# A two-branch diffusion trunk: where the second attention's scores, maxima and first exponential stand between the gate's pieces, and one wait in the last layer's pair products

## The chip, the core and the metric

The kernel runs on one core of one Trainium2 chip. The metric is the device time of one execution in microseconds (us), median of three runs. The core has TensorE (PE in the rows; PEld is its weight load), VectorE (DVE), ScalarE (ACT), GpSimd (POOL) and SyncE (SP), which here only issues DMAs. Each has its own queue of instructions in program order; they wait for each other by semaphores.

## What is computed

Two token streams (512 latent and 128 context tokens, 640 columns in the kernel) pass through two layers. A layer has one combined input projection, four branches (latent attention, gated DeltaNet, Hyena convolution, differential attention), a sigmoid gate for each branch and channel, a projection, a residual, and an MLP. The parts that the change touches, cut from the reference:

```python
def _diff_attend(q, k, v, lam):          # the second attention: two maps for each head
    ...
        s1 = jnp.einsum('bqhd,bkhd->bhqk', qb[..., 0, :], k1).astype(jnp.float32) * scale
        s2 = jnp.einsum('bqhd,bkhd->bhqk', qb[..., 1, :], k2).astype(jnp.float32) * scale
        p = jax.nn.softmax(s1, axis=-1) - lam * jax.nn.softmax(s2, axis=-1)
        return jnp.einsum('bhqk,bkhd->bqhd', p.astype(v.dtype), v)

def _gated_merge(branches, z_gate, w_branch, w_out):
    stacked = jnp.stack(branches, axis=2)
    proj = jnp.einsum('blnc,ncd->blnd', stacked, w_branch)
    gates = jax.nn.sigmoid(z_gate.reshape(bsz, seq, N_BRANCH, D_MODEL))
    return jnp.einsum('bld,de->ble', jnp.sum(gates * proj, axis=2), w_out)

def _trunk_layer(x, p, l, cond, ctx):
    ...
    x = x + gt_m * (jnp.square(jax.nn.relu(h @ p['mlp_w1'][l])) @ p['mlp_w2'][l])
```

## The kernel before, in words

**Attention and gates share one stretch.** The two attentions are cut into 40 units, each one head and one tile of 128 queries: units 0 to 19 are the first attention (one map of scores), units 20 to 39 the second (two maps). Two units of one tile (an even and an odd one, two neighbouring heads) make a pair; the last tile of each five is the context's, with 128 columns of scores instead of 640 (units 18 and 19, 28 and 29, 38 and 39). A unit v goes through the engines so: PE multiplies queries and keys (`score`; for two maps twice two matmuls into the two halves of `ps_aux`, L1708, or L1705 for a context unit); DVE takes each map's maximum (`row_max`, L3065); ACT takes each map's exponential with its sum (`exp`, L2288); DVE scales and combines them (`combine`, L3074 for one map, L3081 to L3086 for two); PE transposes the result (`turn`, L1723); ACT copies it out of `ps_dense` (`turned`, L2298); and after each odd unit PE multiplies both with the values (`values`, L1735).

**Between these stand the gate's pieces.** 22 of the 32 gate blocks are computed inside the attentions. A block i has five pieces (i, 0) to (i, 4), called `gate_part`: pieces 0 to 3 are 12 matmuls of 320 columns each (L1035), piece 3 also the rows of the modulation (L1061), and piece 4 turns those rows (L1068) and projects a branch (L1657). On ACT a block has a copy of the projection's weights (L2055, at piece 1), a copy of the next block's weights (L2050, at piece 2) and the tanh of the gate (L2276, at piece 3); on DVE it has the copy of the rows (L3193, at piece 3), which L1068 reads, and the product of gate and projection (L3046, at piece 4), which frees the bank for the next block's piece 0. In the second attention each pair carries one block: pieces 0 and 1 in the even unit's step, 2 and 3 in the odd unit's, 4 behind it. The order is written by hand, in one loop on each engine; a helper only says which pieces stand in which step.

**What a step of unit v holds.** On PE: the pieces, then `score(v + 1)`, then `turn(v)`; only where an even unit's step holds a piece 4 does the score come first, which never is the case in the second attention. On ACT: the pieces, the first map's exponential of v + 1, `turned(v)`, the second map's exponential of v + 1. On DVE: the pieces, `row_max(v + 1)`, `combine(v + 1)`.

**What a score waits for.** Each map of unit v + 1 overwrites the half of `ps_aux` that the same map of unit v used, so it waits for that map's exponential:

```python
                                pe.wait_ge(*exps.nth(l, U + 2 * u - 1 + m))
```

It also waits for its tile's queries, which SP loads (L773) after the weights of a later gate block (L752), when piece 4 of the pair two places before is done.

**The MLP's pairs.** In the MLP, 14 pairs of hidden blocks in each layer are computed by seven quadrant products each (`quadrant_pair`), with operands split into high and low parts. In the even pairs (seven of the 14) a function `early` is called between products 4 and 5; in the first layer it computes rows of the next layer's modulation, in the last layer it returns at once. Ahead of the call PE waits for the low part of operand A22, which product 7 needs; DVE makes it (L3300). Products 5 to 7 wait for DVE's sums of the quadrants (L3327 and after).

Of the kernel before, what the change touches and what calls it, by code (L numbers as in the profile page):

```python
# [23 lines left out]
DEPTH = 2  # L24
# [147 lines left out]
def trunk(nc, ins, outs, links):  # L172
    ctx = ExitStack()
    with ctx:
# [96 lines left out]
        parts = sums  # L271
# [225 lines left out]
        U = NT * H  # L497
# [208 lines left out]
        def has_branch(parts):  # L706

            return any(q % 5 == 4 for q in parts)
# [312 lines left out]
        def _(pe):  # L1021
# [660 lines left out]
            def attention(l):  # L1682
# [78 lines left out]
                for w in range(U):  # L1761
                    for v in (2 * w, 2 * w + 1):
                        parts = parts_ahead(3 * w + v % 2)
                        score_first = v % 2 == 0 and has_branch(parts)
                        if score_first:
                            score(v + 1)
                        for q in parts:
                            gate_part(l, q)
                        if v + 1 < 2 * U and not score_first:
                            score(v + 1)  # L1770
                        turn(v)
                    for q in parts_ahead(3 * w + 2):
                        gate_part(l, q)
                    values(w)
# [162 lines left out]
            def mlp_group(l, g):  # L1937
# [19 lines left out]
                        dense_split(dense_banks(j % 2), j % 2, h_high, h_low, block_low(l, 0, j))  # L1957
                for p in range(first_pair(g), (g + 1) * GROUP_PAIRS):
                    i = p % GROUP_PAIRS
                    quadrant_pair(l, p, (lambda: early(i // 2)) if i % 2 == 0 and (g or i) else None)  # L1960
                last_pair = (g + 1) * GROUP_PAIRS - 1
                for m in range(KC):
                    pe.wait_ge(*block_high(l, g, KC + m))
# [51 lines left out]
        def _(act):  # L2015
# [262 lines left out]
            def attention(l):  # L2278
# [40 lines left out]
                a(q_high.bitcast(F32R), d_q, ACT.Copy).then_inc(parts_ready.sem, 1)  # L2319
                for w in range(U):  # L2320
                    for v in (2 * w, 2 * w + 1):
                        for q in parts_ahead(3 * w + v % 2):
                            gate_part(l, q)
                        two = v + 1 < 2 * U and FU[v + 1][0] == 2
                        if two:
                            exp(v + 1, 0)
                        turned(v)
                        if v + 1 < 2 * U:
                            exp(v + 1, 1 if two else 0)
                    for q in parts_ahead(3 * w + 2):  # L2330
                        gate_part(l, q)
# [224 lines left out]
        def _(dve):  # L2556
# [499 lines left out]
            def attention(l):  # L3056
# [46 lines left out]
                for w in range(U):  # L3103
                    for v_ in (2 * w, 2 * w + 1):
                        parts, behind = parts_ahead(3 * w + v_ % 2), parts_ahead(3 * w + 2)
                        score_first = v_ % 2 == 0 and has_branch(parts)
                        if score_first:
                            row_max(v_ + 1)
                        for q in parts:
# [519 lines left out]
```

## Time and profile before

| | |
|---|---|
| median of 3 runs | 2722.15 us (2717.51 to 2723.63) |
| profiled execution, its own time | 2714.22 us |
| its span | 2712.4 us |
| PE busy | 2593.4 us (96%) |
| PEld busy | 2415.4 us (89%) |
| DVE busy | 1373.8 us (51%) |
| ACT busy | 981.1 us (36%) |
| POOL busy | 666.5 us (25%) |
| PE's share of the chain that ended last | 83% |

Busy is the time in which an engine had an instruction under way, as a share of the span. The profiled execution took 2714.22 us, 7.93 us less than the median of the runs and 3.29 us less than the fastest of them; a sum made from its rows is a difference, and is added to the median. The chain that ended last follows the work back from the last instruction, at each step to what released it.

### The profile page before, as it was taken

The numbers are of one execution on the slowest core, as the hardware profiler recorded it, in microseconds if no ns is written. First come the engines' busy times: TensorE is split into PE (matmuls) and PEld (weight loads), VectorE is DVE, ScalarE is ACT, GpSimd is POOL, SyncE is SP. The second block draws the span as 40 slices with busy tenths as digits, with TensorE's granted clock in tenths as the row PEclk, the third lists the DMA queues.
The fourth block names the chain that finished last, engine by engine and source line by source line (L and its number), as shares of the span: only waits on it lengthen the run. The fifth ranks groups of instructions, "written<-read, shape, count | busy, mean of one in ns | idle before, by whom it ended". The sixth has DMA issues, their size and how long they took to land.

```text
span 2712.4 us, 55055 instructions
## 1 busy us (share of the span) xinstructions
PE 2593.4 (96%) x23766; PEld 2415.4 (89%) x23766; DVE 1373.8 (51%) x2295; ACT 981.1 (36%) x1590; POOL 666.5 (25%) x525
## 2 busy tenths in 40 slices
PE   5998999999999999999999989999999999999997
PEld 5887897889899999999988888888898998999997
DVE  5767624236633646255575775342464347364364
ACT  4251043334422534253341511443344226253352
POOL 2322122222233220211323311322222331211202
PEclk8999999999999999999999999999999999999999
DMA  8110012433343123222330100134332431122222
GB/s 347 40 55 3 3 59 87 142 107 104 108 131 128 63 92 111 83 97 102 131 132 32 48 4 11 62 120 130 99 115 100 143 105 63 63 86 79 74 83 78
DMA packets 73148, 245.38 MB, mean 90 GB/s; under 512 B 7828, under 2 KB 20276, under 8 KB 71888
## 3 DMA queue, kind: packets, MB, share of 16 engines
q1 hardware_dynamic: 69936, 218.21, 23.7%
q0 software_dynamic: 2976, 23.69, 2.4%
q8 instruction: 189, 3.10, 0.5%
q14 instruction: 47, 0.39, 0.0%
HBM read 224.66 MB, written 17.20 MB: 89 GB/s over the span
## 4 chain that ended last, share of the span: by engine, by line
PE 83%; DVE 6%; ACT 5%; issue 3%; DMA 1%; POOL 0%; SPq 0%; DVEq 0%; ACTq 0%; POOLq 0%
PE ps_dense L1027 29%; PE ps_dense L1035 17%; PE ps_dense L1890 5%; PE ps_aux L1027 4%; PE ps_dense L1657 3%; PE ps_dense L1894 3%; PE ps_aux L1421 2%; PE ps_dense L1735 1%; PE ps_aux L1657 1%; PE ps_aux L1711 1%; PE ps_dense L1061 1%; PE ps_aux L1407 1%; PE ps_dense L1723 1%; PE ps_aux L1373 1%; DMA arena<-in_w_early 1%
## 5 line engine op out<-in xcount | busy, mean ns | idle before, releaser
L857 POOL TENSOR_TENSOR w_low<-w_ring,w_high 128x256 fp32r<-128x256 f32 (+1 forms) x338 | 515.7, 1542 | 1450.6 <-ACT w_high L2050 1444.3
L2050 ACT ACTIVATE w_high<-w_ring 128x1024 fp32r<-128x1024 f32 x200 | 212.1, 1061 | 460.2 <-PE ps_dense L1027 260.5
L1027 PE MATMUL ps_dense<-z_both,w_high 128*128 128x320 f32 x2048 | 312.5, 310 | 0.0
L1027 PEld LDWEIGHTS ps_dense<-z_both,w_high 128*128 128x128 f32 x2048 | 302.6, 188 | 2.1 <-issue 1.6
L1035 PE MATMUL ps_dense<-h_high,w_high 128*128 128x320 f32 x1024 | 242.2, 318 | 7.1 <-DVE x_res L3043 3.1
L1035 PE MATMUL ps_dense<-h_high,w_low 128*128 128x320 f32 x1024 | 233.2, 309 | 0.0
L1035 PE MATMUL ps_dense<-h_low,w_high 128*128 128x320 f32 x1024 | 232.5, 308 | 0.0
L3187 DVE SCALAR_TENSOR_TENSOR x_res<-ps_dense,mod,x_res 128x320 f32<-128x320 f32 (+2 forms) x192 | 72.6, 434 | 292.2 <-PE ps_dense L1027 292.2
L1027 PE MATMUL ps_dense<-h_high,w_high 128*128 128x320 f32 x864 | 204.5, 318 | 14.8 <-ACT h_high L2091 11.4
L1027 PE MATMUL ps_dense<-h_low,w_high 128*128 128x320 f32 x864 | 186.8, 309 | 0.0
L1035 PEld LDWEIGHTS ps_dense<-h_high,w_high 128*128 128x128 f32 x1024 | 167.8, 188 | 14.5 <-issue 12.6
L1035 PEld LDWEIGHTS ps_dense<-h_low,w_high 128*128 128x128 f32 x1024 | 171.1, 188 | 0.0
L1035 PEld LDWEIGHTS ps_dense<-h_high,w_low 128*128 128x128 f32 x1024 | 171.0, 188 | 0.0
L1027 PEld LDWEIGHTS ps_dense<-h_high,w_high 128*128 128x128 f32 x864 | 146.1, 192 | 27.5 <-issue 13.8
L1027 PE MATMUL ps_dense<-z_both,w_low 128*128 128x320 f32 x1024 | 160.6, 309 | 0.0
L1027 PEld LDWEIGHTS ps_dense<-z_both,w_low 128*128 128x128 f32 x1024 | 152.8, 188 | 0.0
L1027 PE MATMUL ps_dense<-h_high,w_low 128*128 128x320 f32 x864 | 147.6, 313 | 0.0
L3193 DVE COPY rows_kept<-ps_dense 128x128 f32<-128x128 f32 x64 | 18.7, 292 | 247.1 <-ACT stage L2276 132.4
L1027 PEld LDWEIGHTS ps_dense<-h_low,w_high 128*128 128x128 f32 x864 | 141.7, 188 | 0.3 <-issue 0.3
L1027 PEld LDWEIGHTS ps_dense<-h_high,w_low 128*128 128x128 f32 x864 | 134.1, 191 | 0.0
L3065 DVE TENSOR_REDUCE att_s<-ps_aux 128x1 f32<-128x640 f32 (+1 forms) x120 | 82.2, 713 | 83.3 <-PE ps_aux L1711 40.6
L1890 PE MATMUL ps_dense<-h_low,w_high 128*128 128x320 f32 x392 | 117.9, 312 | 0.0
(528 smaller groups left out, 5084.5 us busy)
## 6 DMA issues: line engine op xcount, KB each, us to landing
w_ring<-in_w_mlp SPq DMA_DIRECT2D x128, 512.0 KB, 3.6
w_ring<-in_w_gate SPq DMA_DIRECT2D x64, 640.0 KB, 3.9
w_ring<-in_w_late SPq DMA_DIRECT2D x64, 512.0 KB, 4.9
w_ring<-in_w_in SPq DMA_DIRECT2D x48, 512.0 KB, 3.5
w_ring<-in_w_out SPq DMA_DIRECT2D x16, 512.0 KB, 3.5
w_ring<-in_w_early SPq DMA_DIRECT2D x16, 512.0 KB, 3.5
arena<-in_dft POOLq DMA_DIRECT2D x2, 2944.0 KB, 14.9
x_kept<-x_res POOLq DMA_DIRECT2D x2, 2560.0 KB, 11.9
```

The costliest lines, as they stand in the source:

```text
L857: last = g.tensor_tensor(w_low[:, n % 2, k:k + step], ring[:, slot, k:k + step, :], w_high[:, n % 2, k:k + step].bitcast(F32), ALU.subtract)
L1027: last = mm(out[:, s, 0:HALF], w_[:, par_, k, :], x_[:, k, s * HALF:(s + 1) * HALF], start=first, stop=final)
L1035: last = mm(out[:, s, 0:HALF], w_[:, par_, k, :], x_[:, k, s * HALF:(s + 1) * HALF], start=k == 0 and x_ is x_high and w_ is w_high, stop= ...
L1061: last = mm(out[32 * (k % 4):32 * (k % 4) + 32], cond_pad[:, k, at:at + 32], tiles[:, k, :], start=j == 0 and k < 4, stop=j == of - 1 and ...
L1373: return mm(psA[to, 2 * i, u * 64:(u + 1) * 64], lt[s % 3][rows(r), d, hh, rows(r)], mv, start=True, stop=True)
L1421: last = mm(out, wm[i][at, u], mv, start=not moved, stop=True)
L1657: last = mm(out[:, s, 0:HALF], w_[:, k, :], x_[:, k, s * HALF:(s + 1) * HALF], start=n == 0 and k == 0, stop=n == 2 and k == 1)
L1890: mm(out, w_[:, k // 2, k % 2], src[:, k], start=fresh and k == 0 and n == 0, stop=False, skip_group_check=True)
L1894: last = mm(out, rest[:, k // 2, k % 2], b_high[:, k], start=False, stop=k == 3, skip_group_check=True)
L2050: a(w_high[:, n % 2], ring[:, j, 0:KC, :], ACT.Copy).then_inc(w_high_in.sem, 1)
L3065: v.tensor_reduce(small_[:, 2 * m, u:u + 1], src, AX.XY if len(src.shape) == 3 else AX.X, ALU.max, negate=True).then_inc(negmax.sem, 1)
L3187: last = v.scalar_tensor_tensor(out=dst[:, p:q], in0=ps, scalar=gate[:, s:s + 1], in1=dst[:, p:q], op0=ALU.mult, op1=ALU.add)
```

## The change

In the second attention the step of every unit is put in another order, on three engines. PE computes `score(v + 1)` ahead of the gate's pieces of step v, for v from 19 to 38; DVE takes the maxima of unit v + 1 ahead of its pieces; ACT takes the first map's exponential of unit v + 1 ahead of its pieces. In the last layer, `quadrant_pair` gets no `early` function, and so PE no longer waits for A22's low part between products 4 and 5. No instruction is added and none removed but that wait.

```diff
@@ TensorE, attention
                         parts = parts_ahead(3 * w + v % 2)
-                        score_first = v % 2 == 0 and has_branch(parts)
+                        score_first = U <= v + 1 < 2 * U or v % 2 == 0 and has_branch(parts)
                         if score_first:
                             score(v + 1)
                         for q in parts:
@@ TensorE, mlp_group
                     i = p % GROUP_PAIRS
-                    quadrant_pair(l, p, (lambda: early(i // 2)) if i % 2 == 0 and (g or i) else None)
+                    quadrant_pair(l, p, (lambda: early(i // 2)) if i % 2 == 0 and (g or i) and l + 1 < DEPTH else None)
@@ ScalarE, attention
                     for v in (2 * w, 2 * w + 1):
-                        for q in parts_ahead(3 * w + v % 2):
-                            gate_part(l, q)
                         two = v + 1 < 2 * U and FU[v + 1][0] == 2
                         if two:
                             exp(v + 1, 0)
+                        for q in parts_ahead(3 * w + v % 2):
+                            gate_part(l, q)
                         turned(v)
@@ VectorE, attention
                         parts, behind = parts_ahead(3 * w + v_ % 2), parts_ahead(3 * w + 2)
-                        score_first = v_ % 2 == 0 and has_branch(parts)
+                        score_first = U <= v_ + 1 < 2 * U or v_ % 2 == 0 and has_branch(parts)
                         if score_first:
                             row_max(v_ + 1)
```

**PE, from an even unit's transposes to the odd unit's pieces.** These are PE's rows in the second attention's second pair (units 22 and 23) before. The four L1708 are the scores of the odd unit, two matmuls for each map; the L1723 are the transposes of the even unit; the L1035 begin piece 2. `exps` is the semaphore of the exponentials, `stacked_queries_in` that of the loaded queries.

```order
L1708 MATMUL ps_aux<-z_both,q_stack_odd 128x320 [waits exps,stacked_queries_in,stacked_keys_in]
L1708 MATMUL ps_aux<-z_both,q_stack_odd 128x320
L1708 MATMUL ps_aux<-z_both,q_stack_odd 128x320 [waits exps]
L1708 MATMUL ps_aux<-z_both,q_stack_odd 128x320
L1723 MATMUL ps_dense<-con,arena 128x128 [waits probabilities_ready,pv_in,pt_in]
L1723 MATMUL ps_dense<-con,arena 128x128 x4
L1035 MATMUL ps_dense<-h_high,w_high 128x320 x2
```

And the same place of the changed kernel:

```order
L1723 MATMUL ps_dense<-con,arena 128x128 [waits probabilities_ready,pv_in,pt_in]
L1723 MATMUL ps_dense<-con,arena 128x128 x4
L1708 MATMUL ps_aux<-z_both,bout_low 128x320 [waits exps,stacked_queries_in,stacked_keys_in]
L1708 MATMUL ps_aux<-z_both,bout_low 128x320
L1708 MATMUL ps_aux<-z_both,bout_low 128x320 [waits exps]
L1708 MATMUL ps_aux<-z_both,bout_low 128x320
L1035 MATMUL ps_dense<-h_high,w_high 128x320 x2
```

The odd unit's scores have left this place for the start of the even unit's step, and the scores of the next pair's even unit (queries in `bout_low`) now stand directly behind the transposes, with pieces 2 and 3 behind them instead of ahead of them.

**PE, from the modulation's rows to their transpose.** The same pair before, at the end of piece 3 (L1061) and the start of piece 4 (L1068):

```order
L1061 MATMUL ps_dense<-w_ring,cond_pad 32x128 x7
L1708 MATMUL ps_aux<-z_both,bout_low 128x320 [waits exps,stacked_queries_in,stacked_keys_in]
L1708 MATMUL ps_aux<-z_both,bout_low 128x320
L1708 MATMUL ps_aux<-z_both,bout_low 128x320 [waits exps]
L1708 MATMUL ps_aux<-z_both,bout_low 128x320
L1723 MATMUL ps_dense<-con,arena 128x128 [waits probabilities_ready,pt_in]
L1723 MATMUL ps_dense<-con,arena 128x128 x4
L1068 MATMUL ps_dense<-con,rows_kept 128x2 [waits modulation_rows_in,gate_act]
```

Changed:

```order
L1061 MATMUL ps_dense<-w_ring,cond_pad 32x128 [waits ring_in3]
L1061 MATMUL ps_dense<-w_ring,cond_pad 32x128 x7
L1723 MATMUL ps_dense<-con,arena 128x128 [waits probabilities_ready,pt_in]
L1723 MATMUL ps_dense<-con,arena 128x128 x4
L1068 MATMUL ps_dense<-con,rows_kept 128x2 [waits modulation_rows_in,gate_act]
```

Between L1061 and L1068, which waits for tanh (`gate_act`) and the rows' copy (`modulation_rows_in`), only the transposes are left.

**ACT, one pair.** Before, from piece 1 on; `negmax` is DVE's maximum:

```order
L2055 ACTIVATE w_proj_high<-w_ring 128x256 [waits block_done]
L2288 ACTIVATE arena,att_s<-ps_aux,att_s 128x640 [waits negmax]
L2298 ACTIVATE arena<-ps_dense 128x640 [waits pv_ps,pt_ps]
L2288 ACTIVATE arena,att_s<-ps_aux,att_s 128x640 [waits negmax]
L2050 ACTIVATE w_high<-w_ring 128x1024 [waits block_done,ring_in0]
L2276 ACTIVATE stage<-ps_dense 128x640 [waits proj_used,gate_ps]
```

Changed:

```order
L2055 ACTIVATE w_proj_high<-w_ring 128x256 [waits block_done]
L2298 ACTIVATE arena<-ps_dense 128x640 [waits pv_ps,pt_ps]
L2288 ACTIVATE arena,att_s<-ps_aux,att_s 128x640 [waits negmax] x2
L2050 ACTIVATE w_high<-w_ring 128x1024 [waits block_done,ring_in0]
L2276 ACTIVATE stage<-ps_dense 128x640 [waits proj_used,gate_ps]
```

The first exponential has gone ahead of L2055, and the next unit's first exponential stands ahead of the weights' copy L2050; the copy out of `ps_dense` (L2298) and the second exponential keep their order to each other.

## Rows read from the trace of the kernel before

**Rows 1.** Busy time by engine in most of the first layer's second attention.

```profile
core 0: us, PE busy (x) PEld busy (x) DVE busy (x) ACT busy (x) POOL busy (x), PEclk, DMA share, GB/s
614.00:748.00 134.00, 130.78 (x1098) 121.64 (x1096) 82.26 (x180) 57.96 (x126) 39.07 (x50) 1.00 0.32 107
```

**Rows 2.** Who waited for whom, 600 to 755: us in total, times, longest.

```profile
PE ps_dense L1068 <- DVE rows_kept L3193: 2.3, 5, 1.0
PE ps_dense L1035 <- DVE rs L3046: 1.3, 2, 0.6
```

**Rows 3.** Timeline, second attention: start, duration, engine, instruction, [idle before it].

```profile
646.19 1.56 DVE L3065 TENSOR_REDUCE att_s<-ps_aux 128x1 f32<-128x640 f32 x2 [1.57 <-PE ps_aux L1708]
646.29 0.71 PE L1723 MATMUL ps_dense<-con,arena 128*128 128x128 f32 x5
646.75 0.54 PE L1035 MATMUL ps_dense<-h_high,w_high 128*128 128x320 f32 x2
647.05 0.80 ACT L2288 ACTIVATE arena<-ps_aux,att_s 128x640 f32<-128x640 f32 x1 [5.21 <-DVE att_s L3065]
...
647.84 0.70 ACT L2298 ACTIVATE arena<-ps_dense 128x640 f32<-128x640 f32 x1
...
648.42 0.80 ACT L2288 ACTIVATE arena<-ps_aux,att_s 128x640 f32<-128x640 f32 x1
...
649.19 1.07 ACT L2050 ACTIVATE w_high<-w_ring 128x1024 fp32r<-128x1024 f32 x1
...
649.34 0.16 DVE L3084 RECIPROCAL att_s<-att_s 128x1 f32<-128x1 f32 x1 [0.62 <-ACT arena L2288]
...
649.79 0.89 DVE L3086 SCALAR_TENSOR_TENSOR arena<-arena,att_s 128x640 f32<-128x640 f32 x1
...
650.45 0.64 PE L1061 MATMUL ps_dense<-w_ring,cond_pad 128*32 128x128 f32 x16
...
651.02 0.86 PE L1708 MATMUL ps_aux<-z_both,q_stack_odd 128*128 128x320 f32 x4
651.16 0.70 ACT L2276 ACTIVATE stage<-ps_dense 128x640 f32<-128x640 f32 x1 [0.90 <-PE ps_dense L1061]
...
651.89 0.29 DVE L3193 COPY rows_kept<-ps_dense 128x128 f32<-128x128 f32 x1 [1.22 <-ACT stage L2276]
...
652.33 0.35 PE L1068 MATMUL ps_dense<-con,rows_kept 128*128 128x2 f32 x2
...
655.73 0.56 PE L1035 MATMUL ps_dense<-h_high,w_high 128*128 128x320 f32 x2
```

**Rows 4.** SP's load of queries: one issue, and the eight loads' time to landing.

```profile
641.81 0.38 SPq L773 DMA_DIRECT2D q_stack_odd<-q_parts  x1
...
DMA to landing us min/median/max: 5.0/5.8/6.6
```

**Rows 5.** Timeline at the context's units, where the second attention begins.

```profile
605.94 0.54 PE L1035 MATMUL ps_dense<-h_high,w_high 128*128 128x320 f32 x2
...
606.93 0.16 DVE L3074 RECIPROCAL att_s<-att_s 128x1 f32<-128x1 f32 x1 [0.53 <-ACT par L2288]
...
614.73 0.53 PE L1035 MATMUL ps_dense<-h_high,w_high 128*128 128x320 f32 x2 [0.64 <-DVE rs L3046]
```

**Rows 6.** Timeline, last layer's MLP: A22's low part, and where product 5 starts.

```profile
2508.54 0.69 DVE L3300 TENSOR_TENSOR con_reused<-w_ring,par_reused 128x512 fp32r<-128x512 f32 x1
...
2513.73 0.49 DVE L3327 TENSOR_TENSOR flow<-flow,ps_dense 128x320 f32<-128x320 f32 x1
...
2514.32 0.39 PE L1890 MATMUL ps_dense<-h_high,w_high 128*128 128x320 f32 x1 [0.95 <-issue]
```

**Rows 7.** Last layer's first pair, start of product 5, and the stretches behind it.

```profile
2296.56 0.38 PE L1890 MATMUL ps_dense<-h_high,w_high 128*128 128x320 f32 x1 [2.35 <-issue]
...
2297.70:2301.00 3.30, 3.30 (x14) 3.30 (x14) 2.25 (x4) 1.89 (x3) 0.00 (x0) 0.50 0.90 309
2302.00:2305.30 3.30, 3.30 (x24) 3.30 (x24) 2.52 (x5) 1.51 (x4) 0.00 (x0) 1.00 0.02 9
```

## The prediction, on record before the changed kernel ran

> **What bounds the kernel now.** I read the windows first, then PE's waits, then the timeline. The window over the first layer's second attention shows PE with an instruction under way for 130.78 of 134.00 us, at full granted clock, while DVE has 82.26 and ACT 57.96 [rows 1]: PE sets the pace, and whatever makes PE stand still or puts nothing in place of a moved matmul is time. The waits say how little there is to win here. In 155 us, PE waited 2.3 us for the copy of the modulation's rows (five times) and 1.3 us for the gate's product on DVE (twice) [rows 2]. With both layers that is 7.2 us, and all of PE's idle time in the window, 134.00 - 130.78 = 3.2 us, says about the same. The timeline of one pair then shows how PE came to wait so seldom [rows 3]: it is always busy with a piece of the gate while DVE and ACT work on the softmax. Each map of a unit takes one maximum on DVE and one exponential on ACT, and ACT has the copy out of ps_dense between the two exponentials.
>
> **The change in the odd unit's step: the scores lose their cover.** Take the pair in [rows 3]. The even unit's transposes start on PE at 646.29, and piece 2 at 646.75. In the changed order the scores of the next pair's even unit stand between these two. Their second map overwrites the half of ps_aux that the odd unit's second exponential reads, so PE waits for that exponential, and it stands on ACT behind the copy of the very transposes that PE has just made. The chain, from rows:
>
> - transposes end: 646.29 + 0.71 = 647.00 [rows 3]. ACT starts some 0.05 us behind an end on PE (L1061 ends at 650.45 + 0.64 = 651.09, and its tanh starts at 651.16), so the copy starts at 647.05 rather than at 647.84, where the first exponential held it up;
> - the second exponential starts 648.42 - 647.84 = 0.58 us behind the copy's start [rows 3], so at 647.63;
> - its result is released 649.34 - 648.42 = 0.92 us after its start (DVE's L3084 waits for just that) [rows 3], so at 648.55;
> - PE needs 0.05 more and half a score. A whole score takes 651.02 to 651.6, about 0.6 us with what stands ahead of L1723, so piece 2 starts near 648.9.
>
> Piece 2 would start at 648.9 instead of 646.75, which is 2.15 us later. Of this about 0.3 us is the first map's half, 0.3 the second's, and 1.55 is PE standing still.
>
> **Is that given back where the scores used to be?** Before, they stood between the modulation's rows (L1061, at 650.45) and the transpose of those rows (L1068, at 652.33). That distance is 1.88 us [rows 3], and it is not made of PE's work: L1061 takes until 651.09, tanh starts at 651.16 and takes 0.70, the copy of the rows starts at 651.89 and takes 0.29, and PE follows. The scores and transposes only just filled it, with what remained appearing as the five waits of 2.3 us in all [rows 2]. Without the scores PE has 0.6 us less to do there and waits 0.6 us longer; the distance stays 1.88. So nothing comes back, and a pair is longer by the full 2.15 us.
>
> **The even unit's step.** The odd unit's scores now stand ahead of pieces 0 and 1 instead of behind. What they wait for, the even unit's second exponential, was already done before: the projection and the values lie between, 652.33 to 655.73 [rows 3]. No wait, no gain, except at the two places in each layer where PE waits 0.64 us for the gate's product ahead of piece 0 because the values of a context pair are short [rows 5]. There the scores (0.6) fill the wait. That is 0.6 us won, twice in each layer.
>
> **Maxima and the first exponential.** They come earlier and are not what PE waits for: the first exponential of the odd unit started at 647.05, and DVE can start the maximum as soon as its queue lets it. What the move puts at risk is what stands behind the exponential on ACT, the weights' copy L2050 and tanh L2276. In the odd step the combination on DVE (L3084 to L3086: 0.45 + 0.89) runs after the release at 648.55, to 649.9; the maximum and the exponential's start take 647.05 - 646.19 = 0.86 more, to 650.8; the exponential 0.8, to 651.6, and the weights' copy 1.07, to 652.7. The rows (L1061) are now made at 648.9 + 3.7 = 652.6 (650.45 - 646.75 = 3.7), so tanh is wanted at 653.3. It fits with 0.6 us to spare: cost nothing, and if that cover is gone, each us beyond it costs one us a pair. POOL makes the low weights behind L2050, which ended at 650.26, 5.5 us before the next block's piece 0 at 655.73 [rows 3]; now it ends at 652.7 and that piece comes near 658, again more than 5 us. SP's queue keeps its order and all its transfers.
>
> **The queries.** A pair's queries are loaded behind piece 4 of the pair two places before: issued at 641.81, landed 5.8 us later at 647.6 (the eight loads take 5.0 to 6.6) [rows 4]. The new place asks for them at 646.75, so the first map now waits for a DMA that was hidden: to 647.6, less than the 648.55 of the second map's wait. Only the slowest loads reach past it: 6.6 us gives 648.4 plus the first half's 0.3, 0.15 us late. I count 0.2 us a layer.
>
> **The context's units and the first one.** Unit 28 and unit 38 have scores of 128 columns, behind full exponentials: 2.0 us each. Unit 30's scores stand behind the short unit 28; the exponential is early and the queries decide (0.9 us by the short chain, 2.15 by the long): 1.5. The very first, unit 20's scores, stand behind unit 18's transposes and wait for unit 19's exponential, which is released at 606.93 where piece 2 began at 605.94 [rows 5]: 1.0 us, and 0.6 for the scores, whose old place is one of those 1.88 us: 1.6.
>
> **The last layer's pairs.** PE's wait for A22's low part ends with DVE's L3300 at 2508.54 + 0.69 = 2509.2, and PE gets to it near 2513.4 and waits until 2514.32 for the first quadrant sum, DVE's L3327, 2513.73 + 0.49 = 2514.22 [rows 6]. The idle 0.95 us has another cause, and the removed wait was long satisfied. Worth nothing, in all seven pairs.
>
> **The sum.** For a layer: six full units (22, 24, 26, 32, 34, 36) by 2.15 = 12.9; two context scores by 2.0 = 4.0; 1.5; 1.6; 0.2 for queries; less 1.2 won. That is 19.0, and 38.0 us for two layers, on a profiled execution of 2714.2 which gives 2752.2. The median of the runs shown stands 7.9 us above that execution: 2722.15 + 38 = 2760. The unknown in it is how late each hand-over between PE and ACT is; 0.1 us either way on two hand-overs for each of 20 stalls is 4 us. The likeliest case's own range is 2753 to 2768. A measurement of this kernel can tell about 0.2%, 5.4 us, from no change.
>
> **Rivals.**
> - *The clock falls.* PE stood still once for 2.35 us, between 2294.2 and 2296.5, and the granted clock was then 0.50 (1.2 of 2.4 GHz) from 2297.70 to 2301.00: 14 matmuls in 3.30 us, where 24 passed at 1.00 [rows 7]. Ten matmuls lost are 3.30 x 10/24 = 1.4 us. After a wait of 0.95 us no fall is seen [rows 6, 1]. Mine are 1.55 us with 0.3 us of matmuls ahead and transposes before that, between the two. If each of 20 stalls brought the fall: 28 us more, 2788. For it: the new stalls are longer than any in this stretch. Against: matmuls stand densely on both sides. Chance 10%, part of the stalls only (2770 to 2788) in most of that. [...]
> - *Tanh comes late.* If the maximum of the next unit comes more than 0.6 us later than I have it, the first exponential and the weights' copy hold up tanh, the rows' transpose and piece 4. One us beyond is one us in each of 16 pairs of both layers: 2776. For it: DVE is the busiest of the helpers, 82.26 of 134 us [rows 1]. Against: the slack worked out above. Chance 7%.
> - *Not slower.* The second map's exponential would have to be released by the time PE has done the first half, 647.05, instead of 648.55; then the scores cost nothing in their new place, and the filled waits show, 1.2 us a layer, and at the most all of PE's 7.2 us of waits: 2715 to 2720. It decides at a release before 647.1, that is, if ACT's second exponential did not need the copy of the transposes ahead of it. In the order of ACT it stands behind it, which speaks against. Chance 5%.
> - *The stall is smaller*, because part of the 1.88 us is PE's work after all and comes back: 0.6 x 16 = 10 us less, 2750. For it: PE's waits for the rows are only 2.3 us. Chance 8%.
>
> The likeliest case holds the remaining 70%. The range reaches from the smaller stall to tanh late: 2747 to 2778. Faster by over 0.2%: 2%; within 0.2%: 3%; slower: 95%.
>
> **What the changed kernel's profile would show.** PE idle ahead of the second half of L1708 in the odd steps, about 1.5 us, released by ACT's L2288; its idle time in the stretch up from 3.2 us to above 20; L1068's wait for L3193 near 0.7 us in every pair; the distance L1061 to L1068 still 1.88; the wait of 0.64 us ahead of piece 0 gone; granted clock 1.00 throughout; the MLP's waits unchanged, 0.95 us ahead of product 5. A pair takes 2.15 us more. Wrong would be the prediction if L1068 or tanh moved by their own, or if the second exponential stood ready when PE reached it.

## The result

The changed kernel takes 2768.86 us, the median of 4 runs (2759.49 to 2776.35); the kernel before took 2721.22 us beside it (4 runs, 2717.51 to 2723.63). The ratio is 1.018, with a 95% interval of 1.016 to 1.0199: 47.6 us slower. Forecast were 38 us more and a time of 2760 with a range of 2747 to 2778. The four runs of the changed kernel lie 16.9 us apart, and the slower one is, the lower its mean granted clock: 0.992, 0.991, 0.989 and 0.988 at 2759.49, 2765.84, 2771.88 and 2776.35 us. The profiled execution is the second of them, 3.0 us below the median.

**The page of the changed kernel.** Its head and its first part, busy time by engine:

```profile
span 2764.1 us, 55055 instructions
PE 2606.9 (94%) x23766; PEld 2420.3 (88%) x23766; DVE 1372.0 (50%) x2295; ACT 983.7 (36%) x1590; POOL 663.0 (24%) x525
```

The number of instructions is the same as before, the span is 51.7 us longer. PE is busy for 13.5 us more although it does the same matmuls, and 12.8 us of that lie in the two second attentions. The granted clock is one part of it: in the three pairs where it fell to half (below), PE is busy for 1.9 to 2.1 us more. But in the pairs without a fall, the last one excepted, it is busy for 0.2 to 0.6 us more as well. There the rows ahead of a wait count for longer: one matmul's row lasts some 0.3 us and the next one starts some 0.15 us behind it, so a row that nothing follows shows its whole length. The rest of the 51.7 us, 38.2 us, is PE standing still.

**The first layer's second attention**, the window that answers to [rows 1] (the pairs are longer, so it runs to 768), and the first five rows of PE's waits from 600 to 785, which answer to [rows 2] (us in total, times, longest):

```profile
614.00:768.00 154.00, 134.87 (x1077) 122.28 (x1078) 80.94 (x180) 59.73 (x128) 35.99 (x50) 0.99 0.28 93
```

```profile
PE ps_dense L1068 <- DVE rows_kept L3193: 7.6, 12, 1.0
PE ps_aux L1708 <- ACT arena L2288: 6.2, 5, 2.6
PE ps_aux L1708 <- issue: 2.5, 3, 1.0
PE ps_aux L1705 <- issue: 1.7, 1, 1.7
PE ps_aux L1708 <- DMA z_both<-k_parts: 1.4, 1, 1.4
```

PE stands still for 154.00 - 134.87 = 19.1 us here; before it was 3.2. Two kinds of wait are new. The scores (L1708, and L1705 for the context) now wait in front of the odd units' pieces, and the rows' transpose L1068, which waited five times before, waits in every pair.

**One pair** as the timeline shows it, beside [rows 3]:

```profile
652.83 0.38 SPq L773 DMA_DIRECT2D q_stack_odd<-q_parts  x1
...
656.36 0.80 ACT L2288 ACTIVATE arena<-ps_aux,att_s 128x640 f32<-128x640 f32 x1 [5.70 <-DVE att_s L3065]
...
657.27 0.71 PE L1723 MATMUL ps_dense<-con,arena 128*128 128x128 f32 x5
...
658.02 0.70 ACT L2298 ACTIVATE arena<-ps_dense 128x640 f32<-128x640 f32 x1 [0.47 <-PE ps_dense L1723]
...
658.62 0.79 ACT L2288 ACTIVATE arena<-ps_aux,att_s 128x640 f32<-128x640 f32 x1
658.62 0.53 PE L1708 MATMUL ps_aux<-z_both,q_stack_odd 128*128 128x320 f32 x2 [0.64 <-issue]
...
659.55 0.56 PE L1708 MATMUL ps_aux<-z_both,q_stack_odd 128*128 128x320 f32 x2 [0.39 <-ACT arena L2288]
659.95 0.46 PE L1035 MATMUL ps_dense<-h_high,w_high 128*128 128x320 f32 x2
```

Read it from the transposes. They end at 657.98, the copy of them (L2298) starts at 658.02, the second exponential 0.60 us behind it, and 0.93 us after that PE may overwrite the second half of `ps_aux`, at 659.55. Piece 2 follows at 659.95, which is 2.68 us behind the start of the transposes; in [rows 3] it was 0.46. The first half waits as well, until 658.62. That is 5.79 us behind SP's issue at 652.83, so the queries had just landed. Here it costs nothing, since the second half would wait until 659.55 anyway.

**Pair by pair.** From the start of one pair's values (L1735) to the next, the changed kernel minus the one before, in us (the name is that of the even unit whose scores stand in the odd step of that stretch; "unit 22's pair" below means its row here):

| scores of | forecast | first layer | second layer |
|---|---|---|---|
| unit 20 | 1.6 | 1.68 | 1.68 |
| unit 22 | 1.55 | 5.59 | 5.59 |
| unit 24 | 2.15 | 2.14 | 2.13 |
| unit 26 | 2.15 | 2.09 | 2.09 |
| unit 28 (context) | 2.0 | 1.96 | 1.96 |
| unit 30 | 1.5 | 1.68 | 1.62 |
| unit 32 | 1.55 | 1.73 | 3.82 |
| unit 34 | 2.15 | 2.16 | 2.12 |
| unit 36 | 2.15 | 2.13 | 2.13 |
| unit 38 (context) | 2.0 | 2.14 | 1.97 |
| last pair | 0 | 0.01 | 0.01 |
| sum (forecast: with 0.2 for queries) | 19.0 | 23.3 | 25.1 |

Three cells are off, and they hold nearly all of the difference to the forecast. The pair with unit 22's scores, first layer, in the timeline:

```profile
620.87 1.49 DVE L3135 TENSOR_TENSOR bout_low<-bout,con_reused 128x1280 fp32r<-128x1280 f32 x1
621.61 0.71 PE L1723 MATMUL ps_dense<-con,arena 128*128 128x128 f32 x5
622.29 0.82 DVE L3054 TENSOR_TENSOR x_res<-x_res,rs 128x640 f32<-128x640 f32 x1
623.02 1.55 DVE L3065 TENSOR_REDUCE att_s<-ps_aux 128x1 f32<-128x640 f32 x2
623.87 0.79 ACT L2288 ACTIVATE arena<-ps_aux,att_s 128x640 f32<-128x640 f32 x1 [8.60 <-DVE att_s L3065]
...
624.90 0.53 PE L1708 MATMUL ps_aux<-z_both,q_stack_odd 128*128 128x320 f32 x2 [2.58 <-ACT arena L2288]
...
626.48 0.69 PE L1708 MATMUL ps_aux<-z_both,q_stack_odd 128*128 128x320 f32 x2 [1.05 <-ACT arena L2288]
```

Once in each layer DVE splits a branch's output into high and low parts (`split_branch(2)`, L3134 and L3135) behind the first attention's last pair, and a residual sum (L3054) follows. Unit 21's maxima stand behind both in DVE's queue and start at 623.02, 1.41 us after the start of the transposes. So even the first exponential comes late: PE waits 2.58 us for it and 1.05 us for the second. Behind that the granted clock falls, and in the second layer it falls behind unit 32's scores too:

```profile
626.90:630.20 3.30, 3.30 (x15) 3.30 (x14) 2.35 (x3) 1.64 (x3) 0.00 (x0) 0.50 0.00 0
...
2067.30:2070.60 3.30, 3.30 (x14) 3.30 (x14) 1.95 (x3) 1.83 (x3) 0.14 (x1) 0.50 0.00 0
```

```profile
2066.76 1.05 PE L1708 MATMUL ps_aux<-z_both,bout_low 128*128 128x320 f32 x4 [2.06 <-DMA z_both<-k_parts]
```

The last row names the keys' load, but of the loads that this score waits for, the queries' is the late one: SP issued it at 2060.33, 6.4 us before 2066.76, and the four issues of keys behind it are the context's, which unit 32 does not ask for. In the first layer the same wait was 1.43 us (the load issued at 698.67, the scores at 704.47), and no fall came. Here PE waited for 2.06 us, and then the clock was 0.50 (1.2 of 2.4 GHz) for 3.4 us.

**The MLP.** The row that answers to [rows 6], in the same pair, which now comes 51.5 us later:

```profile
2565.85 0.41 PE L1890 MATMUL ps_dense<-h_high,w_high 128*128 128x320 f32 x1 [0.90 <-DVE flow L3327]
```

The idle time is 0.90 us where it was 0.95, and it is now put down to DVE's sum.

**Where the 51.7 us of span lie.** The two second attentions hold 23.3 + 25.1 = 48.4. Some 1.6 us stand before the first of them and 1.5 between the two, in code that the change does not touch. Ahead of the first, the clock fell for three stretches of 3.4 us in this execution and for one in that of before; the long low stretch near the start of both lasted 10.2 us here and 13.6 us there. Between the two attentions the clock was low for 10.2 us in both, and where those 1.5 us come from stays open.

### The profile page after: what moved, and what is told of

It is laid out like the page before. It is cut to its first block, busy times and chain, and to the rows that moved or that the text cites. A ratio compares the mean times of both kernels' runs of the same rounds, so it can differ in the third digit from the quotient of the medians.

```text
span 2764.1 us, 55055 instructions
## 1 busy us (share of the span) xinstructions
PE 2606.9 (94%) x23766; PEld 2420.3 (88%) x23766; DVE 1372.0 (50%) x2295; ACT 983.7 (36%) x1590; POOL 663.0 (24%) x525
## 3 DMA queue, kind: packets, MB, share of 16 engines
q1 hardware_dynamic: 69936, 218.21, 23.3%
## 4 chain that ended last, share of the span: by engine, by line
PE 79%; DVE 7%; ACT 6%; issue 4%; DMA 2%; POOL 1%; SPq 1%; DVEq 0%; ACTq 0%; POOLq 0%
PE ps_dense L1027 29%; PE ps_dense L1035 15%; PE ps_aux L1027 4%; PE ps_dense L1890 4%; PE ps_dense L1657 3%; PE ps_dense L1894 2%; PE ps_aux L1421 2%; PE ps_dense L1735 1%; PE ps_aux L1657 1%; PE ps_aux L1711 1%; PE ps_dense L1061 1%; PE ps_aux L1407 1%; PE ps_aux L1373 1%; ACT flow L2433 1%; PE ps_aux L1708 1%
## 5 line engine op out<-in xcount | busy, mean ns | idle before, releaser
L2050 ACT ACTIVATE w_high<-w_ring 128x1024 fp32r<-128x1024 f32 x200 | 211.8, 1059 | 462.0 <-PE ps_dense L1027 260.5
L1027 PE MATMUL ps_dense<-z_both,w_high 128*128 128x320 f32 x2048 | 312.5, 310 | 0.0
L1027 PEld LDWEIGHTS ps_dense<-z_both,w_high 128*128 128x128 f32 x2048 | 302.6, 188 | 2.1 <-issue 1.6
L1035 PE MATMUL ps_dense<-h_high,w_high 128*128 128x320 f32 x1024 | 241.3, 317 | 4.6 <-DVE x_res L3043 3.1
L1035 PE MATMUL ps_dense<-h_high,w_low 128*128 128x320 f32 x1024 | 234.9, 311 | 0.0
L1035 PE MATMUL ps_dense<-h_low,w_high 128*128 128x320 f32 x1024 | 234.5, 310 | 0.0
L1027 PE MATMUL ps_dense<-h_high,w_high 128*128 128x320 f32 x864 | 203.4, 317 | 16.3 <-ACT h_high L2091 12.7
L1027 PE MATMUL ps_dense<-h_low,w_high 128*128 128x320 f32 x864 | 187.0, 309 | 0.0
L1035 PEld LDWEIGHTS ps_dense<-h_high,w_high 128*128 128x128 f32 x1024 | 170.5, 190 | 8.7 <-issue 6.4
L1035 PEld LDWEIGHTS ps_dense<-h_low,w_high 128*128 128x128 f32 x1024 | 172.9, 190 | 0.0
L1035 PEld LDWEIGHTS ps_dense<-h_high,w_low 128*128 128x128 f32 x1024 | 172.8, 190 | 0.0
L1027 PEld LDWEIGHTS ps_dense<-h_high,w_high 128*128 128x128 f32 x864 | 144.7, 190 | 29.0 <-issue 15.0
L1027 PE MATMUL ps_dense<-z_both,w_low 128*128 128x320 f32 x1024 | 160.6, 309 | 0.0
L3193 DVE COPY rows_kept<-ps_dense 128x128 f32<-128x128 f32 x64 | 18.6, 291 | 283.0 <-ACT stage L2276 168.4
L1027 PEld LDWEIGHTS ps_dense<-z_both,w_low 128*128 128x128 f32 x1024 | 152.8, 188 | 0.0
L1027 PE MATMUL ps_dense<-h_high,w_low 128*128 128x320 f32 x864 | 146.4, 312 | 0.0
L1027 PEld LDWEIGHTS ps_dense<-h_low,w_high 128*128 128x128 f32 x864 | 141.8, 188 | 0.3 <-issue 0.3
L1027 PEld LDWEIGHTS ps_dense<-h_high,w_low 128*128 128x128 f32 x864 | 133.1, 190 | 0.0
L865 POOL TENSOR_TENSOR w_ring_low<-w_ring,w_proj_high 128x256 fp32r<-128x256 f32 x64 | 53.0, 828 | 256.3 <-ACT w_proj_high L2055 256.3
```

Source lines behind the costliest of these rows:

```text
L865: g.tensor_tensor(ring_low[:, at, KC:KC + 2, :], ring[:, at, KC:KC + 2, :], w_proj[:].bitcast(F32), ALU.subtract)\
L1027: last = mm(out[:, s, 0:HALF], w_[:, par_, k, :], x_[:, k, s * HALF:(s + 1) * HALF], start=first, stop=final)
L1035: last = mm(out[:, s, 0:HALF], w_[:, par_, k, :], x_[:, k, s * HALF:(s + 1) * HALF], start=k == 0 and x_ is x_high and w_ is w_high, stop= ...
L2050: a(w_high[:, n % 2], ring[:, j, 0:KC, :], ACT.Copy).then_inc(w_high_in.sem, 1)
```

## The experiments

Where it is not said otherwise, a kernel computes all that the reference asks for. Differences by pair are always against the trace of the kernel before, of one execution each. The edits of the first two sections are shown against the kernel before, the others against the changed kernel, and all are cut to the lines that matter.

### The last layer's pairs alone

```diff
-quadrant_pair(l, p, (lambda: early(i // 2)) if i % 2 == 0 and (g or i) else None)
+quadrant_pair(l, p, (lambda: early(i // 2)) if i % 2 == 0 and (g or i) and l + 1 < DEPTH else None)
```

> The kernel before with the last layer's edit alone: no wait for A22's low part between products 4 and 5. My account: the wait was satisfied some 4 us before PE reached it, so no change, 2721 within 2 us, and PE's idle time of 0.95 us ahead of product 5 stays. Rival, that the wait held PE there: seven pairs by 0.95 us or more, 2714 or less.

Measured: 2718.88 us against 2720.35, ratio 0.9994 (0.9983 to 1.0006). The wait ahead of product 5 is where it was:

```profile
2517.93 0.42 PE L1890 MATMUL ps_dense<-h_high,w_high 128*128 128x320 f32 x1 [0.92 <-DVE flow L3327]
```

This part of the change is worth nothing that can be measured; all the rest is the attention's.

### Only the even units' steps, only the odd units' steps

```diff
-score_first = v % 2 == 0 and has_branch(parts)
+score_first = v % 2 == 0 and U <= v + 1 < 2 * U or v % 2 == 0 and has_branch(parts)
```

The same on DVE, and on ACT the early first exponential for the same steps alone; the second kernel has `v % 2 == 1` in the new term. Both have the MLP's edit.

> The changed kernel with the new order in the even units' steps only; the odd units' steps (where the scores follow the transposes) are as before on all three engines. My account: all the loss is in the odd steps, and the even steps win the wait of 0.64 us ahead of piece 0 at two places in each layer: 2721 - 2.4 = 2719, within 0.2% of before. Rival, that the move itself costs at every unit or that ACT's new order delays the gate: half of the 48 us remains, about 2745.

> The new order in the odd units' steps only. My account: the odd unit's maximum and first exponential start later again, behind the gate's pieces of the even step, so the second exponential is released 0.8 us later than in the changed kernel and PE's stall grows by that: 16 pairs by 0.8 and the 2.4 us won is lost, 2769 + 15 = 2784. Rival, that the clock or the pure move sets the loss: not above 2769.

Measured: even steps only 2720.28 us, ratio 1.0 (0.9991 to 1.001); odd steps only 2781.51, ratio 1.0222 (1.0204 to 1.0239). So the loss sits in the odd step, and the odd step alone is dearer than the whole change: full pairs cost 2.92 us, and 4.4 us where the clock fell. PE waits for both halves, here in unit 26's pair:

```profile
655.41 0.53 PE L1708 MATMUL ps_aux<-z_both,q_stack_odd 128*128 128x320 f32 x2 [1.08 <-ACT arena L2288]
...
656.69 0.90 PE L1708 MATMUL ps_aux<-z_both,q_stack_odd 128*128 128x320 f32 x2 [0.75 <-ACT arena L2288]
```

In the kernel with both parts the odd unit's first exponential is done before the transposes. With the odd part alone its scores stand at the end of the even step, so the exponential starts at 654.39, 0.77 us behind the start of the transposes as in [rows 3], and the copy and the second exponential follow it. The even part thus saves 0.8 us in a full pair, but only beside the odd part.

The even part did give the forecast 0.6 us at unit 32's pair (-0.60 and -0.59), but nothing at unit 22's (+0.12 and +0.13). There PE waits for the combination, which the split of the branch holds up:

```profile
625.69 0.74 PE L1723 MATMUL ps_dense<-con,arena 128*128 128x128 f32 x5 [0.76 <-DVE arena L3088]
```

### The second exponential ahead of the pieces too

```diff
 if two:
     exp(v + 1, 0)
+    exp(v + 1, 1)
 for q in parts_ahead(3 * w + v % 2):
     gate_part(l, q)
 turned(v)
-if v + 1 < 2 * U:
-    exp(v + 1, 1 if two else 0)
+if v + 1 < 2 * U and not two:
+    exp(v + 1, 0)
```

This takes the copy of the transposes out of the chain that PE waits for, and nothing else.

> The changed kernel with the second map's exponential moved up behind the first, ahead of the gate's pieces and of the copy of the transposes. My account: the scores' second half no longer waits; what is left is the queries' landing (0.9 us) and the scores' own 0.6 us: 1.5 instead of 2.15 us in each full pair and less in the first pair, 2769 - 12 = 2757. Rival, that the queries' transfer is the wait that decides: under 3 us won. Rival, that the second exponential is the whole loss: back to about 2725.

Measured: 2755.44 us, ratio 1.0132 (1.0115 to 1.015). The two stretches are 15.7 and 18.6 us longer than before instead of 23.3 and 25.1. In unit 26's pair nothing waits for ACT any more, and all four matmuls of the scores run in one go:

```profile
653.76 0.70 ACT L2298 ACTIVATE arena<-ps_dense 128x640 f32<-128x640 f32 x1
654.08 0.82 PE L1708 MATMUL ps_aux<-z_both,q_stack_odd 128*128 128x320 f32 x4 [0.57 <-issue]
```

What remains is a wait for the queries, issued at 648.37: the scores start 5.7 us later. The full pairs cost between 0.95 and 2.43 us; only the pairs of unit 22, where the maxima come late, cost more, 3.45 and 4.27.

### The queries' load ahead of the weights' loads

```diff
 for i in range(N_GATE):
+    for n in range(2, 2 * NT):
+        if i == gate_behind(U // 2 + n - 2):
+            sp.wait_ge(*s_ps.nth(l, U + 4 * (n - 1)))
+            queries_load(l, n)
     load(l, B_GATE + 2 * i, ins["w_gate"], slice(i, i + 1), 10)
```

The same four lines are gone from behind the two loads; the keys' load stays there. First this alone, then with the early second exponential.

> The changed kernel with each pair's queries loaded ahead of the gate block's weights in SP's queue instead of behind them. My account: the first half of the scores no longer waits for the transfer, but the second half still waits for the second exponential: 0.2 us a layer, 2768. Rival, that the transfer is what decides: 0.9 us in each of 18 pairs, 2752.

> Both: second exponential moved up, and the queries loaded ahead of the weights. My account: neither wait is left, only the scores' 0.6 us for which the gap between the modulation's rows and their transpose was the cover, and the late maximum in each layer's first pair: 2721 + 20 x 0.6 - 2.4 + 5 = 2736. Rival, that some third wait (tanh, the clock) holds: 2750 or more.

Measured: alone 2765.67 us, ratio 1.0169 (1.0149 to 1.0189); with the exponential 2743.82, ratio 1.0093 (1.0072 to 1.0113). Alone it leaves the full pairs at 2.09 to 2.15 us, and takes unit 30's pair from 1.68 to 1.33. With the exponential early it takes the full pairs to 0.94 (unit 32's to 1.15). The scores no longer wait there, so I expected 0.6, the time of the matmuls themselves, and 2736 us in all; it was 7.8 us more. The other 0.3 us of a pair is ACT's:

```profile
653.27 0.79 ACT L2288 ACTIVATE arena<-ps_aux,att_s 128x640 f32<-128x640 f32 x1
...
653.97 0.64 PE L1061 MATMUL ps_dense<-w_ring,cond_pad 128*32 128x128 f32 x16
654.04 1.05 ACT L2050 ACTIVATE w_high<-w_ring 128x1024 fp32r<-128x1024 f32 x1
...
654.99 0.70 ACT L2276 ACTIVATE stage<-ps_dense 128x640 f32<-128x640 f32 x1
...
656.16 0.35 PE L1068 MATMUL ps_dense<-con,rows_kept 128*128 128x2 f32 x2 [0.85 <-DVE rows_kept L3194]
```

Two exponentials now stand ahead of the weights' copy, so tanh starts 0.38 us after its rows are made (654.61) instead of 0.07, and L1068 waits 0.85 us instead of 0.54. Here the rival "tanh comes late" is real, which it is not in the full pairs of the changed kernel.

### The branch's split behind the maxima

```diff
 if score_first:
     row_max(v_ + 1)
+if v_ == U:
+    dve.wait_ge(*pv_in.nth(l, U // 2))
+    split_branch(2)
 for q in parts:
     gate_part(l, q)
...
 take_values(w)
-if w == U // 2 - 1:
-    dve.wait_ge(*pv_in.nth(l, U // 2))
-    split_branch(2)
```

> The changed kernel with DVE's split of the third branch (2.3 us, once a layer) moved from ahead of unit 21's maximum to behind it. My revised account: it held up the maximum, both exponentials and PE in the second attention's first pair, 2.6 us a layer and a fall of the clock of 1.4 us each: 2769 - 8 = 2761. If the split had no part in it: 2769.

Measured: 2758.99 us, ratio 1.0145 (1.0123 to 1.0167). Unit 22's pair costs 2.09 us instead of 5.59, in both layers, and PE's two waits there are 0.19 and 1.05:

```profile
619.94 0.53 PE L1708 MATMUL ps_aux<-z_both,q_stack_odd 128*128 128x320 f32 x2 [0.19 <-ACT arena L2288]
...
621.52 0.56 PE L1708 MATMUL ps_aux<-z_both,q_stack_odd 128*128 128x320 f32 x2 [1.05 <-ACT arena L2288]
```

Most of that pair's excess, 3.5 us, thus comes from the split ahead of the maxima, and no fall of the clock follows. But 2.09 is not the 1.55 of the forecast: tanh is late in this pair as well, and L1068 waits 0.97 us, 0.43 more than elsewhere. The two stretches together gained 4.1 us and not 7, since unit 32's pair now costs 3.82 and 3.88, and unit 30's in the second layer 2.37. So the median came near the 2761 expected by another sum than mine, which is in part luck. At unit 32 the queries come late, and the clock falls right behind:

```profile
699.02 0.82 PE L1708 MATMUL ps_aux<-z_both,bout_low 128*128 128x320 f32 x4 [2.05 <-DMA bout_low<-q_parts]
...
699.90:702.90 3.00, 3.00 (x13) 3.00 (x13) 1.62 (x3) 1.83 (x3) 0.17 (x1) 0.50 0.00 0
```

### Matmuls in the waits

```diff
+if n_maps == 2 and v % 2 == 0:
+    pe.wait_ge(*exps.nth(l, U + 2 * u - 1 if u else U))
+    for _ in range(8):
+        mm(psA[:, 0, 340:340 + P], c_("ones"), c_("ones"), start=True, stop=True)
```

These eight matmuls of 128 columns stand ahead of an even unit's scores, behind the first wait for the exponential and ahead of the queries' wait. Their result is overwritten.

> The changed kernel with 8 matmuls of 128 columns (some 0.12 us each) put in ahead of each even unit's scores, behind the wait for the first exponential and ahead of that for the queries, where PE stands anyway; their result is overwritten. My account: PE's clock fell three times in the two attentions of the profiled execution, 1.4 us each; the filler prevents that and costs little: 2765 to 2769, with less spread. Rival, that the clock is the main loss: 2745 or less.

Measured: 2769.36 us, ratio 1.0183 (1.0163 to 1.0203), the four runs within 3.3 us. The added matmuls cost 0.24 us in a full pair and 1.7 at unit 20. Unit 22's pairs kept their wait (2.49 us) and the fall of the clock behind it (at 627.5 and 1992.9), since the filler stands behind that wait. At unit 32, where the filler lies in the queries' wait, both layers cost 2.15 us and no fall is seen. As a measure of what the clock costs in all, the experiment is inconclusive: what the filler costs hides what it may save.

### Half of the scores ahead

```diff
+halved = score_first and v % 2 == 1
 if score_first:
-    score(v + 1)
+    score(v + 1, (0,) if halved else None)
 for q in parts:
     gate_part(l, q)
+if halved:
+    score(v + 1, (1,))
```

In the odd step only the first map's scores stand ahead of the pieces, the second map's stay where they were, and the same for DVE's maxima.

> The changed kernel, but in the odd units' steps only the first map's half of the scores (and its maximum) stands ahead of the pieces; the second half is back behind the modulation's rows. My account: PE no longer waits for the second exponential, only for the queries' landing, and half of the scores again covers the gap between rows and their transpose: a full pair 1.2 us longer than before instead of 2.15, and 1.4 us less in each layer's first pair: 2769 - 18 = 2751. Rival, that the first half and its queries make the loss: 2765 or more.

Measured: 2749.05 us, ratio 1.0111 (1.0096 to 1.0126). Eight of the ten full pairs other than unit 22's cost 1.17 to 1.46 us instead of 2.13, the other two 1.88 and 2.07. The wait for the second exponential is gone. In unit 26's pair, which cost 1.18, the 0.3 us of the first half and two waits are left, and they make up the 1.2:

```profile
656.94 0.53 PE L1708 MATMUL ps_aux<-z_both,q_stack_odd 128*128 128x320 f32 x2 [0.51 <-issue]
...
662.97 0.35 PE L1068 MATMUL ps_dense<-con,rows_kept 128*128 128x2 f32 x2 [0.38 <-DVE rows_kept L3199]
```

### ACT in its old order

```diff
-two = v + 1 < 2 * U and FU[v + 1][0] == 2
-if two:
-    exp(v + 1, 0)
 for q in parts_ahead(3 * w + v % 2):
     gate_part(l, q)
+two = v + 1 < 2 * U and FU[v + 1][0] == 2
+if two:
+    exp(v + 1, 0)
 turned(v)
```

> The changed kernel with ACT's order as before (the first exponential behind the gate's pieces); PE's and DVE's new orders stay. My account: the loss comes from PE's place for the scores, and ACT's order neither adds to it nor helps: 2769 within 3 us. Rival, that the exponential ahead of the weights' copy and tanh is part of the loss: 2760 or less. Rival, that it is what keeps the stall short: 2780 or more.

Measured: 2768.12 us, ratio 1.0191 (1.0177 to 1.0206), full pairs 2.12 (but 3.84 and 3.81 at unit 32, both with a fall of the clock). Over the whole kernel, moving the first exponential ahead of the pieces on ACT neither costs nor gives anything that can be measured.

### The even part with the late split

The kernel of the even steps alone, with the split moved as above.

> The new order in the even units' steps only, and DVE's split of the third branch behind unit 21's maximum. My account: in the first pair the late combination of unit 21 (0.76 us of PE's time) goes, and the filled wait of 0.64 us shows there too: with the 0.6 us of the other place, 1.9 us a layer, 3.8 us less than before, 2716; about at the edge of what 12 executions can tell. Otherwise as before, 2720.

Measured: 2716.88 us against 2717.23, ratio 0.9998 (0.9989 to 1.0006). The trace shows the two filled waits in each layer, -0.66 and -0.58 us, and stretches 1.14 us shorter, where I expected 1.9. Over the whole kernel that can't be told from no change. No version here beats the kernel before.

## Why the prediction came out so

**The mechanism was right, and its price in most pairs.** The forecast chain of an odd step had copy, exponential and release at 0.05, 0.58 and 0.92 us from each other; they came at 0.04, 0.60 and 0.93. The pairs of units 24, 26, 34 and 36 measured 2.09 to 2.16 us for 2.15, context scores 1.96 to 2.14 for 2.0. Of the 2.1 us of such a pair PE stands still for 1.6, where I had 1.55. Three experiments bear the cause out. Without the odd part the loss is gone (even steps alone, 1.0). With the copy out of ACT's chain and the queries early a full pair falls to 0.94 us. And with only one map ahead it falls to about 1.2.

**"So nothing comes back" held.** L1061 starts at 647.80 and L1068 at 649.69, 1.89 us apart, as in [rows 3]; L1068 waits in each pair, mostly 0.54 us where I had 0.7 (0.98 in the three pairs of each layer whose own units are the context's):

```profile
647.80 0.64 PE L1061 MATMUL ps_dense<-w_ring,cond_pad 128*32 128x128 f32 x16
...
649.25 0.29 DVE L3193 COPY rows_kept<-ps_dense 128x128 f32<-128x128 f32 x1 [2.69 <-ACT stage L2276]
649.69 0.35 PE L1068 MATMUL ps_dense<-con,rows_kept 128*128 128x2 f32 x2 [0.54 <-DVE rows_kept L3193]
```

The rival of the smaller stall is out by this distance.

**The units at the edges.** Unit 20's and unit 30's scores, estimated at 1.6 and 1.5, measured 1.68 and 1.62 to 1.68.

**The mis-sized term: unit 22's pair.** The sum had it as one of "six full units" less 0.6 us won, 1.55. It measured 5.59 in each layer, 4.0 us more. The step that failed is "DVE can start the maximum as soon as its queue lets it": I never looked at what stood in that queue at the place where the two attentions meet. With the split moved behind the maxima the pair fell by 3.5 us, which shows the cause. That experiment took waits and fall of the clock away together. Apart they can be estimated: a pair with a fall stood 1.5 us above one without in the odd-steps kernel (4.4 against 2.92), which leaves about 2.0 us for the waits. The two kernels with the early second exponential bear out that the wait by itself is the larger part. Their pairs of unit 22 have the same wait of 2.58 us, in the first layer without a fall (3.45 us in both) and in the second with one (4.27 and 4.56). Nor was the 0.6 us won here, for the split holds up the combination; that it comes back without the split is seen in the last experiment (-0.66).

**"Granted clock 1.00 throughout" was wrong in three places.** The rival "The clock falls" was put at the 1.55 us stalls of every pair, and there it does not come true: in the changed kernel none of the eight pairs of units 24, 26, 34 and 36 shows a fall. It came behind the longer waits that I hadn't seen, unit 22's in both layers and unit 32's in the second. The step there is "Only the slowest loads reach past it", counted with 0.2 us. It had slow loads lengthen the wait by 0.15 us each, and nothing for what may follow. In the second layer the scores started 6.4 us behind the load's issue, PE's wait was 2.06 us instead of 1.43, and the clock fell: 3.82 instead of 1.73. With the queries loaded early this pair cost 1.74 us in both layers, with a first wait of 0.19 us and no fall.

**The rest.** The MLP's edit is worth nothing, as worked out from [rows 6]. "Tanh comes late" did not occur in the full pairs, where the slack of 0.6 us held, and shows only when another exponential is put ahead of it. The sum of the terms was 38.0 us, the two stretches gave 48.4: 8.1 us are unit 22's pairs and 2.3 unit 32's in the second layer. By the medians the difference is 47.6. So the time is in the range in part by luck: 2768.86 lies just above the 2753 to 2768 that I gave the likeliest case, and the range reached further only for a late tanh and a partial fall of the clock. The first didn't come; the second came at three places, and the late maxima that led to two of them were in no rival.

## What to carry to other kernels

A score, or any work that overwrites a buffer, is hidden only by what stands between the last read of that buffer and itself. To move it ahead of that work, follow the chain of the reader on its own engine, with the copy or the sum that stands in that queue, and price the move as chain less cover. Then do this again for the pairs at the seams of the loop, where an engine has a one-off in its queue: one such pair in each layer cost as much as two and a half others. And count nothing as won at the place that the work has left, if other engines set its length: here the distance from L1061 to L1068 stayed at 1.89 us with the scores gone from it.

## What the runs showed of the hardware

- The clock's fall is not fixed to a wait. In the second attentions of the changed kernel and of the eight experiments that move the odd scores, longer waits brought it more often: PE stood still in one piece for 2.05 us or more 24 times, and the clock went to 0.50 in 19 of them, mostly in the 2 us behind the wait, in three while PE still stood. Of 19 waits of 1.3 to 1.7 us none was followed by a fall. In the kernel of the odd steps, a pair's two waits of about 1.1 and 0.7 us with half a score between them (1.4 and 0.4 in two pairs) were followed by a fall in four full pairs and by none in six.
- Outside these stretches waits of that length had a fall too, so the 19 make no rule. PE's wait of 1.5 us at L1027 near 1400 us, with one of 0.9 us some 2 us ahead of it, had a fall to 0.50 near it in all 13 traces, which began between 0.4 us before the wait's end and 2.5 us behind it. A wait of 1.55 us at L1407 near 248 us had a fall right behind it in 4 of 13.
- The same wait in code that no kernel here touches, 1.83 us near 269.6 us, was followed by a fall in 9 of 13 traces, and the MLP's first long wait of [rows 7], 2.35 us there, by none in the changed kernel, where it was 2.29. So part of what one profiled execution shows over another, by estimate 1.4 to 1.5 us for each fall (10 matmuls of 24 lost in [rows 7]; 4.4 against 2.92 in the odd-steps kernel), belongs to neither kernel.
- A load of 256 KB of queries stands behind two of weights (640 and 512 KB) in SP's queue. In the four places read here it landed 5.6 to 6.3 us after its issue, and the scores that waited for it started 5.71, 5.79, 5.80 and 6.43 us after it. The last two are unit 32's, in the first and the second layer of the changed kernel, and with the fall of the clock their pairs stand 2.1 us apart.
